# A bidirectional DeltaNet and S5 layer on one core: gate and branch tiles moved between the steps of the S5 blocks, and two branch stages made one

## The chip, the cores and the metric

One core of a Trainium2 chip runs the whole layer in one launch. The metric is the device time of the launch in microseconds. The engines are called PE (TensorE), DVE (VectorE), ACT (ScalarE), POOL (GpSimd) and SP (SyncE, which issues most transfers); a queue called ACTq or SPq in the profile is the instruction queue of that engine. All times below are in microseconds unless marked ns.

## What is computed

1280 tokens of 1024 channels (1024 of the sample, 256 of the prompt) go through one layer. Cut to what the change touches:

```
proj = h @ w_in                                  # qkv, z, b, a, u, gate_a, gate_b
o    = gated_delta(...)                          # 8 heads, two directions
y_a  = o @ w_br_a
y_s  = gelu(s5_fwd(u) + s5_bwd(u) + d * u)       # 64 groups of 16 channels, 64 complex states
y_s  = y_s * sigmoid(y_s @ w_glu + b_glu)
y_b  = y_s @ w_br_b
out  = (sigmoid(gate_a) * y_a + sigmoid(gate_b) * y_b) @ w_out
x    = x + gt1 * out                             # then the SwiGLU part and the last norm
mod  = silu(cond) @ w_ada + b_ada                # six shifts, scales and gates, two conditions
```

## The kernel before

Everything is kept with channels on the 128 partitions and the 1280 tokens along the free dimension. A weight product works on tiles: a tile is 1024 rows by 128 columns of a weight, loaded as f32 (`load_tile`, line 168), split into a bf16 high part by ACT (`split_high`, line 174) and a bf16 low part by POOL (`split_low`, line 179), and multiplied by PE in 72 instructions (`multiply_part`, line 190): 8 slices of 128 rows, three passes (high by high, high by low, low by high), and columns of 512, 512 and 256 tokens, 24 instructions for each of these three chunks of tokens. Two tiles, slot 0 and slot 1, form a pair. Loads, splits and products of a slot wait for one another by semaphores (`w_loaded`, `w_high`, `w_low`, `tile_done`, `tile_read`), so that the split of the next tile of a slot runs while PE multiplies the other slot. Each engine runs its instructions in the order in which they are written.

The phases follow one another: the input with its norm, the decays (`phase_decays`), the heads, S5, branch a, branch b, and the tail (output product, SwiGLU, last norm).

In `phase_decays` PE first multiplies the decay weights (line 656), then, between the steps of the decays, 16 products of adaLN rows (`ada_products`, line 279), whose 1 MB loads (line 271) share three slots; a slot is free when its product is done.

`phase_s5` has two parts. The first multiplies eight tiles of u, and beside them DVE works out the parameters: powers of the state's decay (`pa_re`, `pa_im`), the angle of a chunk of 8 tokens (`e1`), the factors of B and C. PE turns B and C between the first pair of u and the other three (lines 1517, 1527). The second part runs over 16 blocks of four groups. A sequence is cut into chunks of 8 tokens, 128 of the sample and 32 of the prompt. For each block:

- POOL makes tables of the cosine and sine of every chunk's angle by doubling, seven levels from 1 to 64 chunks (lines 1766 to 1781), for the next block; it starts when DVE has finished a block.
- DVE makes the input tables `wt` (lines 1878 to 1881) and the output tables `cc` and `cq` (1889 to 1895).
- PE turns `wt` (1794), ACT copies it into `w1` and `w2` (1850 to 1852), PE multiplies the chunks of u (1803), once for each direction, and makes kernel rows from `cc` (1813 to 1815); ACT copies these (1855), and SP spreads them into a Toeplitz block `m` by eight small transfers (1728).
- For each direction DVE rotates the products by the table (1904, 1905, 1910), runs eight scans (1919), and rotates back into `pq` (1925).
- PE forms the outputs from `m`, `cc` and `cq` (1821 to 1825), ACT copies them out of PSUM (1858), SP stores them.

After the last block SP loads one token of u for each direction (1752), from which the new states are worked out.

`phase_branch_a` multiplies, for each of 8 column tiles, the tile of gate_a and the tile of w_br_a, and beside them loads a slice of y and u, adds d * u, and forms the gelu. `phase_branch_b` multiplies 8 tiles of w_glu, and then, for each of 8 column tiles, the tile of gate_b and that of w_br_b; DVE and ACT form the merged rows. The tail loads x (2081) and begins with w_out.

Of the kernel before, what the change touches and what calls it, by code (L numbers as in the profile page):

```python
# [19 lines left out]
P = 128  # L20
# [30 lines left out]
NC5 = NC5_S + NC5_P  # L51
# [47 lines left out]
def setup(nc, ins, outs, consts, ctx):  # L99
# [49 lines left out]
    K.scratch_u = nc.dram_tensor("scratch_u", [KT, P, L5, NC5], F32, kind="Internal").ap()  # L149
    K.scratch_y = nc.dram_tensor("scratch_y", [KT, P, L5, NC5], F32, kind="Internal").ap()  # L150
# [59 lines left out]
def sources(K):  # L210
# [5 lines left out]
        "branch_a": (lambda j, slot: cols(w["w_br_a"], j, P, 0) if slot else cols(w["w_in"], j, P, GA0), KT),  # L216
        "glu": (lambda j, slot: cols(w["w_glu"], j, 2 * P, slot * P), KT),
        "branch_b": (lambda j, slot: cols(w["w_br_b"], j, P, 0) if slot else cols(w["w_in"], j, P, GB0), KT),
# [373 lines left out]
def phase_decays(K):  # L592
# [3 lines left out]
    with ExitStack() as st:  # L596
# [27 lines left out]
        with K.nc.Block() as block:  # L624
# [25 lines left out]
            def _(pe):  # L650
                pe.wait_ge(s_wl, 1)
                for j, out in ((0, pb), (1, pa)):
                    for k in range(KT):
                        for v, a in ((0, 0), (0, 1), (1, 0)):
                            for c0, cn in CHUNKS:
                                mm = pe.matmul(out[0:64, c0:c0 + cn], wp[:, j, v, k, :], K.hn[:, a, k, c0:c0 + cn],
                                               start=(k, v, a) == (0, 0, 0), stop=(k, v, a) == (KT - 1, 1, 0))
                    mm.then_inc(s_mm, 1)
                for n in range(KT, KT + 4):
                    ada_products(K, pe, n, acc)  # L660
# [4 lines left out]
                for n in range(KT + 4, 2 * KT):  # L665
# [4 lines left out]
                mm.then_inc(s_tr, 1)  # L670
                pe.wait_ge(s_dve, 8)
# [4 lines left out]
                ada_turn(K, pe, 1, trm)  # L676
                for n in range(2 * KT, 3 * KT):
# [36 lines left out]
            def _(dve):  # L714
                dve.wait_ge(s_par, 64)
                dve.wait_ge(s_mm, 2)
                dve.tensor_scalar(s_row[:, :], pa[0:64, 0:T], par[:, 0:1], None, ALU.add).then_inc(s_dve, 2)
                dve.wait_ge(s_act, 1)
# [20 lines left out]
                ada_rows(K, dve, 1, acc)  # L739
# [13 lines left out]
                ada_store(K, dve, 1, trm)  # L753
# [607 lines left out]
def phase_branch_a(K, mg, opairs, ys):  # L1361

    q0 = K.q
    K.q += KT
    with ExitStack() as st:
        sg = K.sb("a_sg", [P, T], stack=st)
        y = K.sb("glu_y", [P, L5, NC5], stack=st)
        u = K.sb("glu_u", [P, L5, NC5], stack=st)
        g = K.sb("glu_g", [P, T], stack=st)  # L1370
        out = [K.ps(f"a_out{s}", [P, 1536], st) for s in range(2)]
        s_o = [K.sem(f"a_o_in_{h}") for h in range(H)]
        s_sg, s_mg = K.sem("a_gate"), K.sem("a_mg")
        s_in, s_v, s_g, s_hi, s_lo = (K.sem("glu_" + n) for n in ("in", "sum", "gelu", "high", "low"))
        with K.nc.Block() as block:  # L1375
            @block.sync
            def _(sync):
                def load_y(j):
                    sync.wait_ge(s_g, j + 1)
                    sync.sem_inc(K.pulse, 1)  # L1380
                    for dst, src in ((y, K.scratch_y), (u, K.scratch_u)):
                        sync.dma_start(dst[:, :, :], src[bass.ds(j, 1)].rearrange("o p t c -> (o p) t c")).then_inc(s_in, 16)

                for h in range(H):
                    sync.dma_start(opairs[:, :, h, :], K.scratch_o[h]).then_inc(s_o[h], 16)
                load_y(0)
                with sync.Fori(1, KT) as j:
                    load_pair(K, sync, q0 + j, "branch_a", j)
                    load_y(j)
                load_pair(K, sync, q0 + KT, "glu", 0)  # L1390

            @block.gpsimd
            def _(pool):
                with pool.Fori(1, KT) as j:
                    low_pair(K, pool, q0 + j, "branch_a")
                low_pair(K, pool, q0 + KT, "glu")

            @block.tensor
            def _(pe):
                with pe.Fori(0, KT) as j:  # L1400
                    multiply_tile(K, pe, q0 + j, 0, out[0], K.hn)
                    for h in range(H):
                        pe.wait_ge(s_o[h], 16)
                    multiply_tile(K, pe, q0 + j, 1, out[1], opairs)

            @block.scalar
            def _(act):
                act.sem_inc(s_g, 1)
                with act.Fori(0, KT) as j:
                    act.wait_ge(s_mg, j + 1)  # L1410
                    wait_tile(K, act, q0 + j, 0)
                    act.activation(sg[:, :], out[0][:, 0:T], ACT.Sigmoid).then_inc(K.tile_read[0], 1)
                    split_high(K, act, q0 + j + 1, 0)
                    act.wait_ge(s_v, j + 1)
                    act.wait_ge(s_lo, j + 1)
                    act.activation(g[:, :].rearrange("p (c t) -> p t c", t=L5), y[:, :, :], ACT.Gelu_apprx_tanh).then_inc(s_g, 1)
                    act.wait_ge(s_g, j + 2)
                    act.activation(one(ys[:, 0, :, :], j), g[:, :], ACT.Copy).then_inc(s_hi, 1)
# [931 lines left out]
```

## Time and profile before

| | |
|---|---|
| median of 3 runs | 4470.55 (4466.76 to 4479.29) |
| profiled execution | 4473.08 |
| its span, first to last instruction | 4471.3 |
| PE busy in the span | 3638.4 (81%) |
| DVE busy | 2032.6 (45%) |
| ACT busy | 1086.6 (24%) |
| POOL busy | 944.5 (21%) |
| mean granted clock of TensorE | 0.897 |

An idle time is put down to the instruction that released the engine. By stage, the span is: input and decays to 186, heads to 2075, S5 parameters to 2243, S5 blocks to 2867, branches a and b to 3417, tail to 4471.

### The profile page before, as it was taken

The numbers are of one execution on the slowest core, as the hardware profiler recorded it, in microseconds if no ns is written. First come the engines' busy times: TensorE is split into PE (matmuls) and PEld (weight loads), VectorE is DVE, ScalarE is ACT, GpSimd is POOL, SyncE is SP. The second block draws the span as 40 slices with busy tenths as digits, with TensorE's granted clock in tenths as the row PEclk, the third lists the DMA queues.
The fourth block names the chain that finished last, engine by engine and source line by source line (L and its number), as shares of the span: only waits on it lengthen the run. The fifth ranks groups of instructions, "written<-read, shape, count | busy, mean of one in ns | idle before, by whom it ended". The sixth has DMA issues, their size and how long they took to land. (4 is left out here: it accounts for less than half of the span.)

```text
span 4471.3 us, 60897 instructions
## 1 busy us (share of the span) xinstructions
PE 3638.4 (81%) x22318; PEld 2423.4 (54%) x22318; DVE 2032.6 (45%) x3325; ACT 1086.6 (24%) x1719; POOL 944.5 (21%) x1059
## 2 busy tenths in 40 slices
PE   5789797979797979796844444699999899999997
PEld 2367574748484848484444444455454455555554
DVE  4366565656565656565279999312311211111112
ACT  3132323232323242322211111133211421111112
POOL 2100000000100001010187787011112311111112
PEclk8799898989898989898867767799999999999998
DMA  5400000000000000002111111321112111111111
GB/s 205 152 5 11 19 11 19 11 19 11 19 11 19 11 19 11 19 1 67 59 26 25 27 28 25 98 84 61 38 42 85 32 39 38 42 38 38 43 33 62
DMA packets 224361, 178.64 MB, mean 40 GB/s; under 512 B 23965, under 2 KB 211406, under 8 KB 220838
## 3 DMA queue, kind: packets, MB, share of 16 engines
q1 hardware_dynamic: 217974, 153.94, 11.7%
q10 hardware_dynamic: 4608, 11.54, 0.7%
q0 software_dynamic: 1584, 10.49, 0.6%
q8 instruction: 132, 2.16, 0.2%
q14 instruction: 63, 0.52, 0.0%
HBM read 144.39 MB, written 27.33 MB: 38 GB/s over the span
## 5 line engine op out<-in xcount | busy, mean ns | idle before, releaser
L179 POOL TENSOR_TENSOR w_pair<-w_raw,w_pair 128x1024 bf16<-128x1024 f32 (+1 forms) x156 | 345.7, 2218 | 2461.0 <-ACT w_pair L174 2461.0
L190 PE MATMUL t_out<-hn,w_pair 128*128 128x512 bf16 (+1 forms) x3168 | 575.8, 345 | 13.5 <-DVE hn L2247 10.6
L190 PE MATMUL bank<-hn,w_pair 128*128 128x512 bf16 (+1 forms) x2304 | 487.0, 360 | 86.0 <-ACTq L1219 71.1
L190 PEld LDWEIGHTS t_out<-hn,w_pair 128*128 128x128 bf16 x3168 | 310.9, 98 | 278.1 <-issue 18.4
L190 PE MATMUL t_out<-ys,w_pair 128*128 128x512 bf16 (+1 forms) x2160 | 401.2, 349 | 24.4 <-DVE ys L2268 14.8
L190 PEld LDWEIGHTS bank<-hn,w_pair 128*128 128x128 bf16 x2304 | 224.9, 102 | 294.6 <-issue 129.7
L190 PEld LDWEIGHTS t_out<-ys,w_pair 128*128 128x128 bf16 x2160 | 213.9, 99 | 210.0 <-issue 32.0
L174 ACT ACTIVATE w_pair<-w_raw 128x1024 bf16<-128x1024 f32 x156 | 162.9, 1050 | 419.0 <-PE t_out L190 321.4
L1821 PE MATMUL s_banks<-u_block,m_block 128*128 128x160 f32 x128 | 41.0, 414 | 250.0 <-DVEq L1927 250.0
L2264 DVE TENSOR_TENSOR t_sq<-t_out,t_sq 128x1280 f32<-128x1280 f32 x22 | 32.8, 1492 | 463.7 <-PE t_out L190 463.7
L190 PE MATMUL b_out<-ys,w_pair 128*128 128x512 bf16 (+1 forms) x1152 | 210.8, 345 | 4.0 <-PEq L1375 4.0
L1035 PE MATMUL bank<-xi,mt 128*128 128x128 f32 x1600 | 197.2, 281 | 20.3 <-DVE xi L1289 13.3
L1048 PE MATMUL bank<-xti,vi 128*128 128x128 f32 x1600 | 206.1, 275 | 0.0
L1035 PEld LDWEIGHTS bank<-xi,mt 128*128 128x128 f32 x1600 | 188.9, 196 | 25.9 <-DVE xi L1289 15.0
L1048 PEld LDWEIGHTS bank<-xti,vi 128*128 128x128 f32 x1600 | 192.1, 192 | 0.0
L1161 ACT ACTIVATE gk<-bank,head_scalars 128x128 f32<-128x128 f32 x160 | 45.6, 368 | 535.2 <-PE bank L1027 535.2
L1087 PE MATMUL bank<-u,kd 128*128 128x256 f32 x320 | 108.2, 421 | 79.4 <-DVE u L1319 79.4
L2036 DVE SCALAR_TENSOR_TENSOR merged<-t_out,mod,merged 128x1024 f32 (+1 forms) x48 | 40.2, 880 | 287.7 <-PE t_out L190 267.6
L1299 DVE TENSOR_TENSOR vi<-bank,level_t 128x512 f32<-128x512 f32 x200 | 138.2, 691 | 69.5 <-PE bank L1035 64.4
L1043 PE MATMUL bank<-vi,xti 128*128 128x128 f32 x1280 | 169.3, 275 | 0.0
L1323 DVE SCALAR_TENSOR_TENSOR state<-state,head_carry,bank 128x128 f32<-128x128 f32 x320 | 97.0, 345 | 158.2 <-PE bank L1087 158.2
L1821 PEld LDWEIGHTS s_banks<-u_block,m_block 128*128 128x128 f32 x128 | 30.0, 273 | 253.9 <-DVEq L1927 253.9
(366 smaller groups left out, 6305.8 us busy)
## 6 DMA issues: line engine op xcount, KB each, us to landing
w_raw<-in_w_in SPq DMA_DIRECT2D x56, 512.0 KB, 4.1
w_ada_rows<-in_w_ada SPq DMA_DIRECT2D x24, 1024.0 KB, 6.4
w_raw<-in_w_gu SPq DMA_DIRECT2D x44, 512.0 KB, 3.8
w_raw<-in_w_down SPq DMA_DIRECT2D x16, 512.0 KB, 4.0
scratch_x<-x_t POOLq DMA_DIRECT2D x1, 5120.0 KB, 18.0
scratch_o<-o_pair ACTq DMA_DIRECT2D x8, 640.0 KB, 3.7
scratch_u<-u_rows ACTq DMA_DIRECT2D x8, 640.0 KB, 2.9
u_block<-scratch_u SPq DMA_DIRECT2D x128, 40.0 KB, 1.8
```

The lines of the kernel that those rows point to most:

```text
L174: act.activation(K.w_pair[:, slot, 0, 0:kt, :], K.w_raw[:, slot, 0:kt, :], ACT.Copy).then_inc(K.w_high, 1)
L179: pool.tensor_tensor(K.w_pair[:, slot, 1, 0:kt, :], K.w_raw[:, slot, 0:kt, :], K.w_pair[:, slot, 0, 0:kt, :], ALU.subtract).then_inc(K.w_l ...
L190: mm = pe.matmul(out[:, c0:c0 + cn], K.w_pair[:, slot, w, k, :], x[:, a, k, c0:c0 + cn], start=i < 3, stop=i >= 9 * kt - 3)
L1035: mm = pe.matmul(b[:, t, :], mt[:, 4 * g + t, :], xi[:, 4 * g + t, :], start=True, stop=True)
L1043: mm = pe.matmul(b[:, t, :], xti[:, 4 * g + t, :], vi[:, 4 * g + t, :], start=True, stop=True)
L1048: mm = pe.matmul(b[:, t, :], vi[:, 4 * g + t, :], xti[:, 4 * g + t, :], start=True, stop=True)
L1087: pe.matmul(b[:, 0:2 * P], kd[:, t, :], u[:, i % 2, :, :].rearrange("p d c -> p (d c)"), start=True, stop=True).then_inc(rd.full, 1)
L1161: act.activation(gk[:, 4 * g + t, :], b[:, t, :], ACT.Copy, scale=hs[:, 3, 4 * g + t:4 * g + t + 1])
L1299: dve.tensor_tensor(vi[:, grp(g), :], b, level[:, l, :].unsqueeze(1).to_broadcast([P, 4, P]), ALU.mult).then_inc(rd.free, 1)
L1323: dve.scalar_tensor_tensor(out=state[:, q, d, :], in0=state[:, q, d, :], scalar=hc[:, d, t:t + 1], in1=b[:, d * P:(d + 1) * P], op0=ALU.mu ...
L1821: pe.matmul(o, m[:, g, :], u[:, slot, g, :], start=True, stop=False, skip_group_check=True)
L2036: i = dve.scalar_tensor_tensor(out=v, in0=out[:, a:a + n], scalar=K.mod[:, bass.ds(j + gate * KT, 1), c:c + 1].rearrange("p o c -> p (o c) ...
```

## The change

It touches four places.

1. `phase_decays`: the 16 products of adaLN rows are issued by PE between the decay weights' products (one after every second slice), and the rest between the later steps; the turned rows are stored earlier.
2. S5 parameters: the start state is turned back by the angle of 64 chunks, for which DVE squares `e1` six times; the copies `pb_re` and `pb_im` go. One column is put between sample and prompt (`PROMPT5`).
3. S5 blocks: the loops are written out. POOL makes tables of 64 chunks instead of 128 (six levels), one block ahead; ACT copies them into tables by position (`positions`: mirrored, with the angle counted from the middle) and makes a table of multipliers with zeros at sequence starts (`decays`), so that DVE runs one scan over all four groups and both sequences for each direction. `cq` is copied from `cc` by ACT. Input tables are made a block ahead. The S5 products use six banks; the other two take weight tiles: 16 tiles of gate_a and gate_b, then 8 of w_br_a, cut into 64 gaps of 48 units (a unit is one instruction of 256 columns), four gaps to a block. ACT puts each finished chunk through a sigmoid, or copies it, and stores it in `scratch_g`. Four gaps (40 to 43) stay empty while the heads' outputs are loaded into `hn`. The token loads at the end are issued in the last block.
4. `phase_branches` takes the place of `phase_branch_a` and `phase_branch_b`: it loads y and u slice by slice, forms the gelu, and multiplies the first two tiles of w_glu slice by slice as it comes; then the other six tiles of w_glu and the 8 of w_br_b. The gates and y_a are loaded from `scratch_g`; POOL multiplies gate_a by y_a. x is loaded here instead of in the tail.

The core of the diff:

```
 # phase_decays, PE
+                        if k % 2:
+                            ada_products(K, pe, KT + 4 * j + k // 2, acc)
-                for n in range(KT, KT + 4):
-                    ada_products(K, pe, n, acc)
 ...
 # S5 parameters, DVE
+                    for _ in range(6):
+                        tt(W(5), W(2), W(2), ALU.mult)
+                        tt(W(6), W(3), W(3), ALU.mult)
+                        tt(W(7), W(2), W(3), ALU.mult)
+                        dve.drain()
+                        tt(W(2), W(5), W(6), ALU.subtract)
+                        dve.tensor_scalar(W(3), W(7), 2.0, None, ALU.mult)
+                        dve.drain()
 ...
 # S5 blocks: where a tile's instructions stand, and the order on PE, ACT, DVE and POOL
+        def start_unit(t, c, i=0):
+            return 120 * t + 48 * c + (1 if c == 2 else 2) * i + (IDLE if t >= GATES else 0)
 ...
+                for b in range(NB):                       # PE
+                    chunk_inputs(b, 0)
+                    fill(4 * b + 1)
+                    if b < NB - 1:
+                        turn_weights(b + 1)
+                    chunk_inputs(b, 1)
+                    fill(4 * b + 2)
+                    fill(4 * b + 3)
 ...
+                    outputs(b)
+                    fill(4 * b + 4)
+                    if b < NB - 1:
+                        kernel_rows(b + 1)
 ...
+                for b in range(NB):                       # ACT
+                    store_chunks(4 * b + 1)
+                    if b < NB - 1:
+                        weights(b + 1)
+                    store_chunks(4 * b + 2)
+                    store_chunks(4 * b + 3)
+                    if b < NB - 1:
+                        positions(b + 1)
+                        decays(b + 1)
+                    read_y(b)
+                    store_chunks(4 * b + 4)
+                    if b < NB - 1:
+                        second_outputs(b + 1)
+                        rows(b + 1)
 ...
+                for b in range(NB):                       # DVE
+                    if b < NB - 1:
+                        input_tables(b + 1)
+                    scan(b, 0)
+                    scan(b, 1)
+                    if b < NB - 1:
+                        output_tables(b + 1)
 ...
+                def scan(b, d):
+                    dve.wait_ge(s.pos, b + 1)
+                    dve.wait_ge(s.x, 2 * b + d + 1)
+                    dve.tensor_tensor(into, xb[:, :, 0:NC5], tcs[:, d, :, 1 - d:1 - d + NC5], ALU.mult)
+                    dve.tensor_tensor(gt[:, :, :], x2b[:, :, 0:NC5], tss[:, d, :, 1 - d:1 - d + NC5], ALU.mult).then_inc(s.xread, 1)
+                    dve.tensor_tensor(into, into, gt[:, :, :], ALU.add)
 ...
+                    dve.tensor_tensor_scan(o, r, v, 0.0, ALU.mult, ALU.add)
 ...
+                for b in range(NB):                       # POOL
+                    more = b + 1 < NB
+                    if more:
+                        first_angles(b + 1)
+                        for n in (1, 2):
+                            double(n)
+                    low_parts(4 * b + 1)
+                    if more:
+                        for n in (4, 8):
+                            double(n)
+                    low_parts(4 * b + 2)
+                    if more:
+                        double(16)
+                    low_parts(4 * b + 3)
+                    if more:
+                        double(32)
+                        pool.drain().then_inc(s.tables, 1)
+                    low_parts(4 * b + 4)
 ...
+                def kernel_rows(b):                       # PE
+                    pe.wait_ge(s.cc, b + 1)
+                    if b:
+                        pe.wait_ge(s.yread, b)
 ...
+                def positions(b):                         # ACT
+                    act.wait_ge(s.tables, b + 1)
+                    if b:
+                        act.wait_ge(s.pq, b)
 ...
 # one stage of branches, PE
+                for k in range(KT):
+                    pe.wait_ge(s_slo, k + 1)
+                    for slot in range(2):
+                        multiply_part(K, pe, slot, out[slot], ys, 9 * k, 9)
+                for j in range(1, KT // 2):
+                    for slot in range(2):
+                        multiply_tile(K, pe, q0 + j, slot, out[slot], ys)
+                for j in range(KT):
+                    if j == 0:
+                        pe.wait_ge(s_lo, KT)
+                    multiply_tile(K, pe, q1 + j // 2, j % 2, out[j % 2], ys2)
 ...
+                def load_slice(k):                        # SP
+                    if k >= 2:
+                        sync.wait_ge(s_g, k - 1)
+                    for dst, src in ((y, K.scratch_y), (u, K.scratch_u)):
+                        sync.dma_start(dst[k % 2], src[k]).then_inc(s_in[k % 2], 16)
```

## Rows read from the trace of the kernel before

**Rows 1.** Busy time by stage: bounds, length, engines (instructions), clock, DMA share, GB/s.
```profile
2075.00:2243.00 168.00, 127.34 (x646) 68.90 (x645) 58.21 (x156) 37.96 (x77) 17.09 (x8) 0.84 0.29 87
2243.00:2867.00 624.00, 290.35 (x1674) 265.42 (x1675) 525.54 (x901) 61.84 (x129) 446.50 (x752) 0.69 0.11 24
2867.00:3417.00 550.00, 526.57 (x2881) 283.54 (x2882) 123.57 (x72) 144.54 (x116) 91.87 (x40) 0.98 0.22 67
```

**Rows 2.** Waits, 2260 to 2830: who waited for whom, total, times, longest.
```profile
PE s_banks L1821 <- DVEq L1927: 250.0, 16, 17.4
```

**Rows 3.** Timeline of POOL: start, length, engine, line, operation; a weight split, one block's tables.
```profile
2113.07 2.12 POOL L179 TENSOR_TENSOR w_pair<-w_raw,w_pair 128x1024 bf16<-128x1024 f32 x1 [109.58 <-ACT w_pair L174]
...
2510.64 0.11 POOL L1766 MEMSET rot_cos<- 128x8 f32 x1 [5.40 <-DVEq L1927]
...
2524.13 0.30 POOL L1775 TENSOR_TENSOR rot_tmp<-rot_cos 128x64 f32<-128x64 f32 x1
...
2533.73 1.04 POOL L1775 TENSOR_TENSOR rot_tmp<-rot_cos 128x512 f32<-128x512 f32 x1
...
2546.80 0.11 POOL L1766 MEMSET rot_cos<- 128x8 f32 x1 [5.40 <-DVEq L1927]
```

**Rows 4.** Timeline of PE: the first w_br_b pair's start and the tail's first tile.
```profile
3196.55 16.00 PE L190 MATMUL b_out<-hn,w_pair 128*128 128x512 bf16 x72 [8.05 <-DVE ys L2019]
...
3416.89 43.41 PE L190 MATMUL t_out<-ys,w_pair 128*128 128x512 bf16 x229 [9.64 <-PEq L160]
```

**Rows 5.** Timeline of PE: transposes of a block, outputs of the last block, its end.
```profile
2482.40 1.04 PE L1794 MATMUL s_banks<-ident,wt 128*128 128x128 f32 x8
...
2827.04 0.90 PE L1821 MATMUL s_banks<-u_block,m_block 128*128 128x160 f32 x2 [9.67 <-DVEq L1927]
...
2829.86 0.66 PE L1821 MATMUL s_banks<-u_block,m_block 128*128 128x160 f32 x2
...
2831.44 0.43 PE L1821 MATMUL s_banks<-u_block,m_block 128*128 128x160 f32 x2
...
2832.80 0.43 PE L1821 MATMUL s_banks<-u_block,m_block 128*128 128x160 f32 x2
...
2852.90 7.16 PE L1838 MATMUL s_banks<-rot_tmp,ones 1*128 1x512 f32 x8 [18.58 <-DMA rot_tmp<-scratch_u]
```

**Rows 6.** Timeline of DVE: a long scan of the decays, then one S5 block.
```profile
135.14 2.81 DVE L723 TENSOR_TENSOR_SCAN c_row<-restart_t,s_row 32x1280 f32<-32x1280 f32 x1
...
2516.47 0.76 DVE L1891 TENSOR_TENSOR cq<-c,pa_re 128x576 f32 x1
...
2526.02 0.69 DVE L1904 TENSOR_TENSOR g_tmp<-s_banks,rot_cos 128x512 f32<-128x512 f32 x1 [2.14 <-PE s_banks L1803]
...
2539.20 0.69 DVE L1904 TENSOR_TENSOR g_tmp<-s_banks,rot_cos 128x512 f32<-128x512 f32 x1
...
2546.29 0.28 DVE L1925 TENSOR_TENSOR pq<-g_scan_p,rot_sin 128x128 f32<-128x128 f32 x1
```

**Rows 7.** Groups of ACT in the S5 blocks: count, busy, mean ns, idle before.
```profile
L1850 ACT ACTIVATE w<-s_banks 128x512 f32<-128x512 f32 x32 | 19.4, 608 | 12.1 <-PE s_banks L1794 10.8
```

**Rows 8.** Timeline of branch a: gelu of a slice, loads of the next, DVE's sum.
```profile
2892.53 2.52 ACT L1416 ACTIVATE glu_g<-glu_y 128x1280 f32<-128x1280 f32 x1
...
2895.75 0.38 SPq L1382 DMA_DIRECT2D glu_u<-scratch_u  x1
...
2900.98 1.55 DVE L1427 SCALAR_TENSOR_TENSOR glu_y<-glu_u,vec,glu_y 128x1280 f32<-128x1280 f32 x1 [1.44 <-DMA glu_u<-scratch_u]
```

**Rows 9.** Timeline of the S5 parameters: one small DVE operation, PE's second transposes.
```profile
2104.45 0.29 DVE L1571 TENSOR_TENSOR e_cos<-s_w 128x128 f32<-128x128 f32 x1
...
2133.91 1.97 PE L1517 MATMUL s_bank<-ident,bn 128*128 128x128 f32 x8 [9.32 <-DVE s_b L1655]
```

**Rows 10.** Timeline of the decays: SP's adaLN loads, PE's last decay product.
```profile
125.10 41.97 SPq L271 DMA_DIRECT2D w_ada_rows<-in_w_ada  x13
...
149.78 4.63 PE L674 MATMUL pb<-end_diag,ones 64*128 64x512 f32 x6 [1.45 <-DVE cum L744]
```

More of the change, by code:

```diff
@@ L670, in _ @@
                 mm.then_inc(s_tr, 1)
+                for n in range(2 * KT + 3, 2 * KT + 6):
+                    ada_products(K, pe, n, acc)
                 pe.wait_ge(s_dve, 8)
@@ L675, in _ @@
                 mm.then_inc(s_tr, 1)
[L676 to L677 removed]
+                for n in range(2 * KT + 6, 3 * KT):
                     ada_products(K, pe, n, acc)
@@ L1356, in _ @@
                 head(H - 1, False)
[L1361 to L1418, printed above, removed]
-                    split_high(K, act, q0 + j + 1, 1)
-            @block.vector
-            def _(dve):
-                dve.sem_inc(s_mg, 1)
-                dve.sem_inc(s_lo, 1)
-                with dve.Fori(0, KT) as j:
-                    dve.wait_ge(s_in, 32 * j + 32)
-                    dve.scalar_tensor_tensor(out=y[:, :, :], in0=u[:, :, :], scalar=K.s5_d[:, bass.ds(j, 1)], in1=y[:, :, :],
-                                             op0=ALU.mult, op1=ALU.add).then_inc(s_v, 1)
-                    dve.wait_ge(s_hi, j + 1)
-                    dve.tensor_tensor(one(ys[:, 1, :, :], j), g[:, :], one(ys[:, 0, :, :], j), ALU.subtract).then_inc(s_lo, 1)
-                    wait_tile(K, dve, q0 + j, 1)
-                    dve.wait_ge(K.tile_read[0], q0 + j + 2)
-                    dve.tensor_tensor(one(mg, j), out[1][:, 0:T], sg[:, :], ALU.mult).then_inc(s_mg, 1)
-                    dve.wait_ge(s_mg, j + 2)
-                    dve.sem_inc(K.tile_read[1], 1)
@@ L1493, in phase_s5 @@
             with nc.Block() as block:
-                stream(K, block, [("u", KT // 2, q0)], "branch_a", before=parameters)
+                stream(K, block, [("u", KT // 2, q0)], "gates", before=parameters)
                 @block.tensor
@@ L1744, in _ @@
[L1744 to L1752 removed]
+                        sync.dma_start(sy[t][:, b * GB:(b + 1) * GB, :], y[t * P_S5:(t + 1) * P_S5, :, :]).then_inc(s.y_out, 16)
@@ new lines, in decays, with weights @@
+                def decays(b):
+                    if b:
+                        act.wait_ge(s.pq, b)
+                    for d in range(2):
+                        for g in range(GB):
+                            j = b * GB + g
+                            i = act.activation(decay[:, d, g, :], keep[:, d, :], ACT.Copy, scale=r8[:, d, j:j + 1])
+                    i.then_inc(s.decay, 1)
+                def weights(b):
+                    act.wait_ge(s.wtr, b + 1)
+                    if b >= 2:
+                        act.wait_ge(s.x, 2 * b - 2)
+                    for d in range(2):
+                        v = turned[:, d, :, :]
+                        act.activation(w1[:, b % 2, d, :, :], v, ACT.Copy)
+                        act.activation(w2[:, b % 2, d, :, 0:64], v[:, :, 64:P], ACT.Copy)
+                        c = act.activation(w2[:, b % 2, d, :, 64:P], v[:, :, 0:64], ACT.Copy, scale=-1.0)
+                    c.then_inc(s.w, 1)
@@ new lines, in _ @@
+                weights(0)
+                positions(0)
+                store_chunks(0)
+                second_outputs(0)
+                rows(0)
+                for b in range(NB):
[12 more added lines that the diff above has]
+                        rows(b + 1)
@@ new lines, in phase_branches @@
+        yy = [tmp[:, 2, :], tmp[:, 3, :]]
+        y = [yu[:, i, 0, :, :] for i in range(2)]
+        u = [yu[:, i, 1, :, :] for i in range(2)]
+        g = sg
+        parts = lambda j: tmp[:, 2:5, :] if j % 2 else tmp[:, 5:8, :]
+        s_in = [K.sem("glu_in_0"), K.sem("glu_in_1")]
+        s_v, s_g, s_shi, s_slo = (K.sem("glu_" + n) for n in ("sum", "gelu", "high", "low"))
+        s_y, s_hi, s_lo = (K.sem("b_" + n) for n in ("y", "high", "low"))
+        s_parts = [K.sem("b_parts_0"), K.sem("b_parts_1")]
@@ new lines, in _ @@
+                for k in range(KT):
+                    q, slot = q0 + k // 2, k % 2
+                    if k >= 2:
+                        act.wait_ge(s_y, k - 1)
+                    wait_tile(K, act, q, slot)
+                    act.activation(sg[slot], out[slot][:, 0:T], ACT.Sigmoid, bias=K.b_glu[:, k:k + 1]).then_inc(K.tile_read[slot], 1)
+                    split_high(K, act, q + 1, slot)
+                    act.wait_ge(s_y, k + 1)
+                    act.activation(ys2[:, 0, k, :], yy[slot], ACT.Copy).then_inc(s_hi, 1)
```

665 lines of the change are left out of this document (419 added, 246 removed).

## The prediction

> **What bounds the kernel now.** I read the busy times by stage first, then the waits and the order of instructions inside the two stages that the change rewrites. Times in us. In the S5 blocks (2243 to 2867, 624 us) TensorE (PE) is busy 290 and VectorE (DVE) 526 [rows 1]. PE's longest wait there is the output product, 250 us in 16 blocks for the end of DVE's scans, and POOL's tables start 36.2 apart, each time on DVE (2510.64, 2546.80) [rows 2, 3]: a block is DVE's chain, with POOL's tables of the next block beside it. Right behind lie 550 us (2867 to 3417) in which PE is busy 527 [rows 1]: 40 weight tiles of 1024 x 128, back to back, 527/40 = 13.2 each; their records end into each other a little, so I take 13.1. So one stage leaves PE free for over 300 us while DVE is full, and the next one uses nothing but PE. The change lays the second over the first; what it can win is read from how much of each is left over.
>
> **The S5 blocks.** *PE's work.* 24 of the 40 tiles move here: 24 x 13.1 = 314. A gap of 48 units is 48/120 of a tile, 5.25. In the last old block five output products of 160 columns take 1.36 at full clock (2831.44 to 2832.80) [rows 5], 0.27 each; a block has 16 input and 20 output products, 9.8. Eight transposes are 1.0 [rows 5]. The kernel rows, four groups of 256 columns, are by columns 4 x 0.43 = 1.7. Together 12.5, and with four gaps 33.5 a block. PE's floor for the stage is 314 + 16 x 12.5 = 514.
>
> *Does DVE fit under it?* Tables: 12 operations where 18 were (the third product pair is now a copy on ACT), 0.76 each [rows 6], 9.1. One direction took 7.4 with POOL idle (2539.20 to 2546.57) [rows 6]. Now it is three operations of 640 elements (0.8), one scan of 648 in place of eight, two products (0.8 each) and a copy. A scan over a full multiplier tensor ran 1280 elements in 2.81 [rows 6], so 1.4; with drains a direction is 5.9. Sum 9.1 + 11.8 = 21, against 33.5. In block time (0 = first input products): inputs 0 to 2.2, gap, transposes, second inputs 8.5 to 10.7, two gaps to 21, outputs to 26.4, gap to 31.7, kernel rows to 33.5. DVE scans from 2.2 and 10.7 and ends near 17; the outputs want it at 21. Four of slack.
>
> *POOL.* Beside DVE six of the seven table levels took 23.1 (2510.64 to 2533.73); the last three of them, mostly beside DVE's waits and PSUM reads, 9.6, and an operation of 64 elements 0.30 [rows 3]. Smaller ones need no more, so the six are at best some 16.6. The seventh level and the copy of B go. Added: 1.5 weight splits a block of 2.12 [rows 3], 3.2. So 20 to 26, under 33.5.
>
> *ACT, and what is queued behind its waits.* Copies of 512 elements take 0.61 [rows 7]. By elements the ten position copies are 3.1, decays 1.6, reading y 0.8, weights 2.4, the second outputs 2.6, rows 1.0, tile and a half 5: 16.5, under 33.5. But ACT's order makes a chain: the position copies wait for POOL's tables, and reading y, which kernel rows wait for, stands behind them. POOL's last level stands behind a split when a tile ends in a block's third gap. That happens in blocks 1, 4, 6, 9 and 12. From 21.0: chunk copy 0.6, high split 1.1 (1024 elements), low split 2.1, last level 4.5 (9.6 shared over three levels by their lengths), positions 3.1, decays 1.6, y 0.8: 34.8 against 31.7, with semaphores a stall of 4. Other blocks lose nothing to 1. I take 4 x 4 = 16 and 9 for the rest and for DVE beside a split.
>
> *The empty gaps.* Gaps 40 to 43 hold no products while the eight heads' outputs (5.2 MB) are loaded into hn. Block 9 still has its 36, block 10 then runs on its own chain: 2.2, 1.6, inputs 2.2, two directions, near 15, outputs, one gap, rows: 27. PE's work in both is 46, so 17 are lost. The Toeplitz copies of block 10 are queued on SP behind the heads' transfers; they have until 15.
>
> *Ends.* Before block 0 tables come first: 5 lost, and the first scan waits for POOL's whole table and ACT's copies, and with them the copy that PE's second transposes want: 6. At the end, PE waited 18.6 for two token loads after the last block [rows 5]; they are now issued early in block 15 behind that block's work. Left are four narrow products (3.7) and 9 for copying, storing y and the barrier.
>
> Sum: 514 + 16 + 9 + 17 + 11 + 4 + 9 = 580, against 624: **-44**.
>
> **One stage in place of two.** Of the 40 tiles 16 stay, 8 of w_glu and 8 of w_br_b. The first two of w_glu can't start before the gelu. They run slice by slice as y arrives. A slice is two loads of 0.64 MB; in the old loop DVE had both 5.2 after the second issue [rows 8] (2895.75 to 2900.98). Then 1.55 on DVE, gelu 2.5 [rows 8] (in two parts 2.7), a copy, a subtraction. Two buffers: a buffer's turn is 5.4 + 1.6 + 2.7 = 9.7, so 4.9 a slice, the bounds being ACT's gelu and copy, 3.9, and no overlap, 9.7. First slice gelu'd at 11, eighth at 45, its halves and products 7 more: pair done at 52 (bounds 45 to 86). Both its tiles end together, so nothing covers the next split: sigmoid 1.5 by elements, splits 1.1 and 2.1, with a table load about 6. Then 6 tiles 79, the old wait of 8 before w_br_b [rows 4] (its end is the same four operations), 8 tiles 105, 2 more for PE's lower clock at the start, and 9.6 to the next stage as before [rows 4]. 262 against 550: **-288**. The gate products on POOL, the loads of parts and of x lie under tiles of 13: the latest part load waits for a merge two tiles back. ACT no longer changes its table twice per tile; that lay beside PE and is worth nothing.
>
> **Before the blocks.** The turned start state adds to DVE's chain of parameters: six squarings of five operations on 128 elements, and some 14 more with a reciprocal; at 0.29 less overlap [rows 9], with drains 6 x 1.3 + 4 = 12, less four copies, 1.4. PE waits for that chain (9.3 on its second group of transposes) [rows 9] and has three tile pairs behind it, so nothing hides it: **+10** (8 to 13). The second copy of u per tile lies beside a tile.
>
> **The adaLN rows.** 13 loads of 1 MB start at 125.10, once PE frees their slots, and last 42 [rows 10]. With products between the decay products the slots come free 26 earlier. What is late next is the decay chain, moved back by 8 products of 1: its last product (149.78 + 4.63) [rows 10] ends at 163, 4 before the old last load is even issued, and that load's landing, 4 or more, drops out of the tail, while two row products move behind the chain: **-8** (0 to -15).
>
> **Sum.** -44 - 288 + 10 - 8 = -330. The profiled execution's span is 4471.3, its own time 4473.1 (1.8 around the span), 2.5 above the median of 4470.6. 4471.3 - 330 + 1.8 - 2.5 = 4140.6; I say **4140**.
>
> **Rivals.** *DVE and POOL take turns.* Where POOL ran its levels of 256 and 512 elements, one direction of DVE took 13.2 (2526.02 to 2539.20) instead of 7.4 [rows 6]. If every POOL operation excludes every DVE operation with both inputs in SBUF, a block needs 9.1 + 1.6 + 2.8 + 3.2 = 16.7 on DVE and 16.6 + 3.2 = 19.8 on POOL, 36.5 one after the other, and with chains around it about 38: the blocks are then 4.5 longer, 16 x 4.5 = 72, 4212. Against it: in the table stretch DVE kept 0.76 while POOL's small operations slipped between. The Trainium skill, SBUF - State Buffer, Who interferes with whom, has this as an exclusive lock that a two-SBUF-input DVE operation and a reading GpSimd operation hold for their whole length, the other one blocked; the trace agrees for the long levels, but not for the small ones, which cost DVE nothing; by the page for all of them the result is the 4212 of this rival.
> *The lower clock.* The granted clock is 0.69 in the old blocks [rows 1], and after 9.7 idle an output group took 2.82 (2827.04 to 2829.86), twice the 1.36 later [rows 5], so it ran at 1.2 GHz and then at 2.4. If the new stage also had 0.69, PE's 514 would be 514 x 0.98/0.69 = 730: 4356. Against it: idle is now 12% of the stage, not half, and stretches as dense as that show 0.98 [rows 1].
> *Loads of slices don't overlap:* pair done at 86 instead of 52, 4174.
> *The fills lengthen the chain instead of filling it.* PE works in order. If each gap stood on the way between a product and the scan that wants it, a block would be the old 36.2 plus four gaps, 57: 912 and 28 for the ends, 360 more than forecast, 4500, slower than before. It decides once DVE's end, now 4 ahead of the outputs, lies behind them by as much as the gaps are long in every block; the schedule above speaks against it.
> *It doesn't do what it says:* the stages overlap less, for instance because splits on POOL come late and PE waits for tiles; that gives between 4212 and 4356.
>
> **How the numbers follow.** Forecast with its own spread (4100 to 4180) 0.58; DVE and POOL in turn (4180 to 4240) 0.19; slices unlapped 0.06; clock or late splits 0.08; series 0.03; better than 4100 (stalls hidden, 25 to 45 of the 66 us that I put on top of PE's floor not there) 0.06. The range 4095 to 4215 leaves out less than 2 in 10. A difference of 0.3% (13 us) is about what a measurement of this kernel can tell from no change. Faster by more: 0.96; within: 0.01; slower by more: 0.03.
>
> **What will show it.** Right: in the S5 stage PE busy above 85%, granted clock above 0.9, blocks 33 to 36 apart except near 36 and 27 for the two around the empty gaps; output products hardly waiting for DVE; PE's kernel rows waiting for ACT in the five named blocks; a first pair of w_glu of about 50. Wrong: output products waiting on DVE in every block (lock), blocks above 38, a clock near 0.7, fills waiting for POOL's weight splits, a first pair of 80.

## The result and the profile after

| kernel | median, us | runs | ratio to before (95% interval) | profiled span |
|---|---|---|---|---|
| before | 4470.95 | 4 (4466.76 to 4479.29) | 1 | 4471.3 |
| changed | 4229.2 | 4 (4224.29 to 4229.91) | 0.9455 (0.9438 to 0.9471) | 4227.4 |

The change makes the kernel 242 us faster, where 330 had been forecast: 4229 against 4140, and 14 above the end of the range. To see where the 88 are, cut both traces at the same events: the first product of the heads, the last product of the heads, POOL's first table of the S5 blocks, ACT's first table load of the branches, and the first product of the tail ([rows 4] has that one for before). First the instruction timeline of the kernel before (start, duration, engine, line, operation; in brackets the idle time ahead of it and what ended it):

```profile
187.86 12.38 PE L190 MATMUL bank<-hn,w_pair 128*128 128x512 bf16 x57 [10.56 <-POOL w_pair L179]
2070.71 4.64 PE L1105 MATMUL bank<-kd,ones 128*128 128x512 f32 x6 [3.57 <-ACT kd L1205]
2243.04 0.11 POOL L1766 MEMSET rot_cos<- 128x8 f32 x1 [0.71 <-DVEq L1929]
2866.84 1.28 ACT L1412 ACT_TABLE_LOAD   x1 [31.70 <-DVEq L1423]
```

and that of the changed kernel:

```profile
182.59 15.60 PE L195 MATMUL bank<-hn,w_pair 128*128 128x512 bf16 x72 [10.68 <-POOL w_pair L184]
2066.53 4.63 PE L1114 MATMUL bank<-kd,ones 128*128 128x512 f32 x6 [3.57 <-ACT kd L1214]
2251.50 0.11 POOL L1789 MEMSET rot_cos<- 128x8 f32 x1 [0.46 <-POOLq L1426]
2918.21 1.28 ACT L2231 ACT_TABLE_LOAD   x1 [6.86 <-PEq L165]
3174.49 1.03 PE L195 MATMUL t_out<-ys,w_pair 128*128 128x512 bf16 x2 [8.41 <-PEq L2158]
```

| stretch | before | after | difference | forecast |
|---|---|---|---|---|
| up to the heads | 187.9 | 182.6 | -5.3 | -8 |
| heads | 1882.9 | 1883.9 | +1.1 | 0 |
| S5 parameters and u | 172.3 | 185.0 | +12.6 | +10 |
| S5 blocks | 623.8 | 666.7 | **+42.9** | **-44** |
| branches | 550.1 | 256.3 | -293.8 | -288 |
| tail | 1054.4 | 1052.9 | -1.5 | 0 |
| sum | 4471.3 | 4227.4 | -243.9 | -330 |

Five of the six come out within 6 us of the forecast, and their errors nearly cancel (-0.9 together). The S5 blocks miss by 87, which is the whole difference. Busy time by stage of the changed kernel, the answer to [rows 1] (stretch, length, then busy time and instructions of PE, PE's weight loads, DVE, ACT and POOL, the granted clock, DMA share and rate):

```profile
2067.00:2251.00 184.00, 132.40 (x652) 71.02 (x651) 67.49 (x194) 40.52 (x87) 17.11 (x8) 0.81 0.27 80
2251.00:2918.00 667.00, 562.09 (x3401) 395.50 (x3401) 379.75 (x442) 252.13 (x545) 350.76 (x665) 0.90 0.28 74
2918.00:3174.00 256.00, 218.35 (x1152) 114.71 (x1152) 116.54 (x64) 79.49 (x66) 67.32 (x24) 0.93 0.45 157
3174.00:4227.00 1053.00, 995.87 (x5460) 542.21 (x5460) 155.00 (x150) 206.58 (x189) 206.97 (x89) 0.97 0.14 41
```

In the blocks PE is now the busiest engine, DVE fell from 526 to 380, and the lower clock is gone (0.90, not 0.69). Still PE stands idle for 105 of 667. Who waits for whom in that stage (engine, what it writes, line, what it waited for; us in total, times, longest):

```profile
POOL w_pair L184 <- ACT w_pair L179: 237.3, 24, 16.9
DVE g_in L2081 <- PE s_banks L1873: 237.0, 29, 17.7
ACT pos_cos L1965 <- POOLq L1825: 128.1, 14, 11.0
PE s_banks L1887 <- ACT y_block L2012: 74.9, 14, 11.3
PE s_banks L1902 <- DVE pq L2099: 9.6, 1, 9.6
```

The output products' wait for DVE, 250 us in the kernel before [rows 2], is down to 9.6, once, in the block with the empty gaps. DVE has slack: 237 us of waiting for PE. In its place PE's kernel rows (L1887) wait for ACT's copy of y (L2012) 14 times, 75 us in all. ACT in turn waits 128 us for POOL's tables (L1965), and POOL 237 us for the high halves of weight tiles (L184), that is, for PE to end a tile. PE waits for ACT, ACT for POOL and POOL for PE: a ring. One turn of it, in block 2 (blocks are counted from 0 throughout):

```profile
2367.16 2.14 POOL L184 TENSOR_TENSOR w_pair<-w_raw,w_pair 128x1024 bf16<-128x1024 f32 x1 [14.09 <-ACT w_pair L179]
2371.28 1.56 POOL L1798 TENSOR_TENSOR rot_tmp<-rot_cos 128x64 f32<-128x64 f32 x1
2381.89 0.89 POOL L1798 TENSOR_TENSOR rot_tmp<-rot_cos 128x256 f32<-128x256 f32 x1
2386.70 0.73 POOL L1801 TENSOR_TENSOR rot_sin<-rot_tmp 128x256 f32<-128x256 f32 x1
2387.58 0.63 ACT L1965 ACTIVATE pos_cos<-rot_cos 128x512 f32<-128x512 f32 x1 [8.36 <-POOLq L1825]
2390.69 2.65 ACT L1982 ACTIVATE scan_decay<-scan_keep,r 128x162 f32<-128x162 f32 x8
2393.25 0.68 ACT L2012 ACTIVATE y_block<-s_banks 128x644 f32<-128x644 f32 x1
2394.08 0.59 PE L1887 MATMUL s_banks<-cc,bst 128*16 128x128 f32 x2 [4.82 <-ACT y_block L2012]
2397.58 3.35 PE L1873 MATMUL s_banks<-u_block,w 128*128 128x161 f32 x16
```

POOL stands 14 us idle with four table levels queued behind a split whose tile isn't done. The split runs, then the levels take 18 us (2369.3 to 2387.4); ACT copies positions and decays; only then comes y, and PE, which has waited 4.82. The wait costs twice. The granted clock in the gap ahead of the wait, in the kernel rows behind it, in the input products behind those, and in the gap's products that follow (same columns as above):

```profile
2384.00:2389.20 5.20, 5.20 (x37) 3.33 (x34) 1.31 (x2) 1.62 (x5) 3.29 (x4) 1.00 0.02 5
2394.10:2397.50 3.40, 3.40 (x24) 2.40 (x24) 0.00 (x0) 2.87 (x4) 1.67 (x1) 0.50 0.47 109
2397.60:2400.80 3.20, 3.20 (x18) 3.16 (x18) 0.00 (x0) 1.47 (x2) 2.63 (x16) 0.72 0.64 145
2401.00:2405.00 4.00, 4.00 (x20) 1.85 (x19) 3.73 (x5) 0.60 (x1) 3.58 (x10) 1.00 0.38 80
```

At 0.50, the lower of the two levels (1.2 GHz), the kernel rows take 3.50 (2394.08 to 2397.58). In block 0, without a wait, they took 1.95 (2265.97 to 2267.92).

### The profile page after: what moved, and what is told of

The parts are those of the page before. It is cut to its first block and busy times, and to the rows that moved or that the text cites. A ratio compares the mean times of both kernels' runs of the same rounds, so it can differ in the third digit from the quotient of the medians.

```text
span 4227.4 us, 59349 instructions
## 1 busy us (share of the span) xinstructions
PE 3593.6 (85%) x22319; PEld 2380.5 (56%) x22319; DVE 1889.9 (45%) x2896; ACT 1212.5 (29%) x2094; POOL 824.3 (19%) x955
## 5 line engine op out<-in xcount | busy, mean ns | idle before, releaser
L184 POOL TENSOR_TENSOR w_pair<-w_raw,w_pair 128x1024 bf16<-128x1024 f32 (+1 forms) x156 | 351.1, 2253 | 2331.7 <-ACT w_pair L179 2331.7
L1853 PE MATMUL s_banks<-hn,w_pair 128*128 128x512 bf16 (+1 forms) x1728 | 321.0, 345 | 0.0
L1853 PEld LDWEIGHTS s_banks<-hn,w_pair 128*128 128x128 bf16 x1728 | 169.7, 98 | 137.0 <-issue 2.7
L1044 PEld LDWEIGHTS bank<-xi,mt 128*128 128x128 f32 x1600 | 194.0, 201 | 29.4 <-DVE xi L1298 19.2
L195 PEld LDWEIGHTS b_out<-ys,w_pair 128*128 128x128 bf16 x1152 | 114.7, 100 | 140.5 <-issue 30.3
```

What stands on the lines that cost most here:

```text
L184: pool.tensor_tensor(K.w_pair[:, slot, 1, 0:kt, :], K.w_raw[:, slot, 0:kt, :], K.w_pair[:, slot, 0, 0:kt, :], ALU.subtract).then_inc(K.w_l ...
L195: mm = pe.matmul(out[:, c0:c0 + cn], K.w_pair[:, slot, w, k, :], x[:, a, k, c0:c0 + cn], start=i < 3, stop=i >= 9 * kt - 3)
L1044: mm = pe.matmul(b[:, t, :], mt[:, 4 * g + t, :], xi[:, 4 * g + t, :], start=True, stop=True)
L1853: mm = pe.matmul(out, K.w_pair[:, slot, wv, k, :], K.hn[:, a, k, c0:c0 + cn], start=i == 0, stop=i == 3 * KT - 1)
```

## Experiments

Three theories. **Queue**: the ring above is the whole shortfall; it is made by what stands ahead of what in POOL's and ACT's in-order queues, and opening it at any one place returns it. **Take turns** (the rival of the prediction): the table levels and DVE's products exclude each other, and the block's period is what the two need. **Clock**: PE is granted less in this stage whatever the waits.

| run | edit to the changed kernel | median, us | ratio to before (95%) |
|---|---|---|---|
| e1 | ACT reads y before positions and decays | 4152.9 | 0.9284 (0.9267 to 0.9300) |
| e2 | ACT reads y between positions and decays | 4195.0 | 0.9375 (0.9358 to 0.9391) |
| e3 | POOL makes all table levels, then splits | 4125.5 | 0.9228 (0.9211 to 0.9244) |
| e4 | DVE's tables left out after the first blocks | 4146.6 | 0.9274 (0.9257 to 0.9290) |
| e5 | e1 and e3 | 4127.7 | 0.9229 (0.9215 to 0.9243) |
| e6 | e3, and the start state turned last | 4113.0 | 0.9199 (0.9187 to 0.9212) |
| e7 | decay phase of the kernel before | 4244.6 | 0.9492 (0.9478 to 0.9507) |
| e8 | e3 and e4 | 4121.3 | 0.9212 (0.9197 to 0.9228) |

**e1: ACT's order.**

```diff
+                    read_y(b)
                     if b < NB - 1:
                         positions(b + 1)
                         decays(b + 1)
-                    read_y(b)
```

> The changed kernel with one exchange in ACT's order: reading y comes before the position copies and the decays of the next block instead of behind them. In the changed kernel PE's kernel rows wait 74.9 us in 14 times for the reading of y, and after such a wait the kernel rows take 3.5 where they took 1.95 in block 0. Theory 'queue' (that wait, predicted in five blocks, is in every block, because y's reading stands on ACT behind copies that wait for POOL's last table level, and it is the whole shortfall): the wait falls from 75 to under 10, kernel rows come back to about 1.95 (14 x 1.55 = 22 us) and the input products behind them by 0.7 each (10 us); ACT's copy of the kernel rows now comes later, so the transposes of the next block may wait some 1 us each. Total 4229 - 65 - 22 - 10 + 15 = about 4147 (4120 to 4170). Theory 'take turns' (DVE and POOL exclude each other and the block's period is what these two need, 38 or more): the wait moves to the position copies and the scans, the period stays near 40 and the time within 15 us of 4229. Theory 'clock' (PE is granted less in this stage whatever the waits): the wait goes but kernel rows stay at 3.5: about 4165 to 4180.

4152.9, 76 less. PE's waits in the blocks:

```profile
PE s_banks L1863 <- ACT k_rows L2006: 23.9, 14, 9.2
PE s_banks L1887 <- ACT y_block L2012: 0.9, 1, 0.9
```

The wait for y is gone. A smaller one took its place: ACT copies the kernel rows later now, and the next block's transposes (L1863), which use the same banks, wait for that (in the changed kernel once, for 6.4). *Take turns* (within 15 of 4229) and *clock* (4165 to 4180) both expected more time than this.

**e2: a smaller dose at the same place.**

```diff
                         positions(b + 1)
-                        decays(b + 1)
                     read_y(b)
+                    if b < NB - 1:
+                        decays(b + 1)
```

> The same place at a smaller dose: reading y is put between the position copies and the decays, so only the eight decays (2.65 us) no longer stand before it. 'Queue': the kernel rows' wait shortens by 2.65 in 14 blocks, 75 to about 38; kernel rows after a shorter wait still begin at the lower clock, so 0 to 12 more: 4229 - 37 = 4192 (4178 to 4196). 'Take turns': within 10 us of 4229, since POOL's tables end no earlier.

4195.0, 34 less for 2.65 us taken out ahead of y. The wait:

```profile
PE s_banks L1887 <- ACT y_block L2012: 44.7, 14, 8.7
```

So time follows what stands ahead of y on ACT nearly one to one: 30 of the wait and 34 of the total.

**e3: POOL's order.**

```diff
                         first_angles(b + 1)
-                        for n in (1, 2):
+                        for n in (1, 2, 4, 8, 16, 32):
                             double(n)
-                    low_parts(4 * b + 1)
...
-                    low_parts(4 * b + 4)
+                    for g in range(4 * b + 1, 4 * b + 5):
+                        low_parts(g)
```

> The changed kernel with POOL's order changed, ACT's as it was: POOL makes all six table levels of the next block first and splits the block's weight tiles behind them; in the changed kernel it stands 237 us in 24 waits for ACT's high halves, that is for PE to end a tile, with two or three table levels queued behind each. 'Queue': tables end some 8 us before reading y is wanted, the kernel rows' wait falls from 75 to under 10, with the clock 4229 - 70 - 30 = about 4130 (4105 to 4160); a split comes up to 15 later, but its tile is wanted only two and a half gaps after its buffer came free, so tiles don't wait. 'Take turns': the levels are as long (22 us or more in all) and now meet the scans and output tables of DVE, which then hold the output products: 4200 or above, with waits of the outputs for DVE's products. If the late splits are what matters, fills wait for POOL: 4230 or slower.

4125.5, 104 less. The busy times of 2300 to 2600 (columns as above), first of this kernel:

```profile
2300.00:2600.00 300.00, 300.00 (x1962) 210.82 (x1961) 205.87 (x245) 138.96 (x293) 186.73 (x374) 1.00 0.33 85
```

and of the changed kernel:

```profile
2300.00:2600.00 300.00, 260.60 (x1603) 182.46 (x1602) 172.14 (x197) 118.59 (x262) 160.66 (x298) 0.92 0.26 67
```

The input products and the kernel rows of the stage, grouped by line (busy time, mean ns of one, idle time ahead), in e3, where their lines are 1863 and 1877:

```profile
L1863 PE MATMUL s_banks<-u_block,w 128*128 128x161 f32 x512 | 79.0, 307 | 0.9 <-DVE c_tmp L2072 0.9
L1877 PE MATMUL s_banks<-cc,bst 128*16 128x128 f32 x128 | 24.5, 273 | 2.9 <-ACT y_block L2002 2.9
```

and in the changed kernel:

```profile
L1873 PE MATMUL s_banks<-u_block,w 128*128 128x161 f32 x512 | 85.9, 324 | 0.9 <-DVE c_tmp L2082 0.9
L1887 PE MATMUL s_banks<-cc,bst 128*16 128x128 f32 x128 | 37.6, 394 | 74.9 <-ACT y_block L2012 74.9
```

The first position copy of a block in the timeline of e3:

```profile
2397.68 0.64 ACT L1955 ACTIVATE pos_cos<-rot_cos 128x512 f32<-128x512 f32 x1 [0.46 <-ACT gate_ring L1938]
```

PE is busy for all 300 us at the full clock. ACT's copy follows its own last copy at once and no longer waits for POOL (8.36 in the turn above); kernel rows wait once, for 2.9, in the last block ahead of the empty gaps; with the wait the slow products went (37.6 to 24.5, 85.9 to 79.0): the clock was a result of the waits, so theory *clock* falls. Blocks stand 33.65 apart (2375.48 and 2409.11 are the starts of two). The stage, from POOL's first table at 2249.04 to ACT's table load at 2811.65, takes 562.6 instead of 666.7.

**e4: the share of contention.** `input_tables(b)` returns after its waits from block 1 on, `output_tables(b)` from block 2 on; that work is left out.

> The changed kernel with part of the work left out: DVE makes its input table for block 0 and its output tables for blocks 0 and 1 only, later blocks use these again; scans and all orders stay. In the changed kernel the last three table levels on POOL take 16 to 17 us a block, most of them beside these DVE operations; where DVE stood idle (block 10 and the first tables) the same three took 8.5 to 9.5. 'Queue' with contention as one of its links: the last level is 2.6 shorter where it alone stands behind a split, two or three levels are 4 to 7 shorter elsewhere, so the kernel rows' wait falls from 75 to some 10 to 25 and the total to 4229 - 57 - 20 = about 4152 (4130 to 4180). If contention is no link of it (the levels are long for another reason), levels stay at 16 and the time within 10 us of 4229.

4146.6, 83 less; the kernel rows' wait is 24.9 in 9 blocks:

```profile
PE s_banks L1887 <- ACT y_block L2012: 24.9, 9, 9.2
```

One operation of POOL's last level, grouped by line and form, 2300 to 2600 (busy time, mean ns), in the changed kernel:

```profile
L1798 POOL TENSOR_TENSOR rot_tmp<-rot_cos,rot_sin 128x256 f32<-128x256 f32 x8 | 8.6, 1074 | 0.0
```

in e4:

```profile
L1798 POOL TENSOR_TENSOR rot_tmp<-rot_cos,rot_sin 128x256 f32<-128x256 f32 x8 | 5.0, 631 | 0.0
```

and in e3:

```profile
L1798 POOL TENSOR_TENSOR rot_tmp<-rot_cos,rot_sin 128x256 f32<-128x256 f32 x9 | 13.2, 1469 | 0.0
```

With DVE's tables out of the way the operation takes 0.63 instead of 1.07. So contention of the two engines is a strong link of the ring: in POOL's old order most of the shortfall needs it. In e3 the same operation is longer still (1.47), and the mean one of that level takes 1.11 (1.00 in the changed kernel, 0.66 in e4), yet e3 is the faster kernel. That contention counts only while the tables are late is what e8 tests. How e4's block 2 runs, with a tile that ends in the same gap as in the turn above (the first and the last operation of POOL's last three levels, then the kernel rows):

```profile
2356.05 1.56 POOL L1798 TENSOR_TENSOR rot_tmp<-rot_cos 128x64 f32<-128x64 f32 x1
2366.33 0.73 POOL L1801 TENSOR_TENSOR rot_sin<-rot_tmp 128x256 f32<-128x256 f32 x1
2373.96 0.39 PE L1887 MATMUL s_banks<-cc,bst 128*16 128x128 f32 x2
```

Three levels take 11.0 there (2356.05 to 2367.06) where they took 16.2 in the turn above (2371.28 to 2387.43), and the kernel rows don't wait at all. (The expectation gives 8.5 to 9.5 for the three levels of the changed kernel where DVE stood idle. By the trace it is 11.2 for the first tables, 2261.58 to 2272.81, and 11.0 for those made around the start of block 10, 2684.55 to 2695.52.)

**e8: the same omission where the ring is open.**

> POOL's tables first, and with the same work left out as in the run without tables: DVE makes its input table for block 0 and its output tables for blocks 0 and 1 only. In POOL's old order this took 83 us. 'Queue' (DVE and POOL lengthening each other matters only through the kernel rows' wait): that wait is already gone, PE is busy all the time in blocks 1 to 8, so leaving the tables out is worth nothing more than the first block's ends, 4125.5 less 0 to 6: 4120 to 4127. 'Take turns' as a cost of its own: some tens of us less, under 4105.

4121.3: the omission that was worth 83 in POOL's old order is worth 4 in the new one, where the intervals of e3's and e8's ratios overlap. As a cost of its own, *take turns* falls.

**e5: both orders.**

> Both remedies at once: POOL makes all table levels before it splits weights, and ACT reads y before the position copies. 'Queue': each alone took the same wait away (75 us of the kernel rows' wait for reading y, to 2.9 and 0.9), so they don't add up: the time is that of POOL's order alone, 4125.5, within 6 us (if ACT's later copy of the kernel rows holds the transposes as it did with ACT's order alone, up to 8 above). If they were two separate causes, about 4050 (4125.5 less 76).

4127.7. Worth 76 and 104 alone, the two together are worth 102: two cuts through one ring.

**e6: the start state.** On top of e3, the lines from `dve.tensor_copy(W(2), e1[0][:, :, :])` to the two writes of `h0` move behind the last subtraction into `b2st`.

> POOL's order as in the run where POOL makes tables first, and one more edit: the turning of the start state (six squarings and what follows, 13.5 us on DVE from 2102.65 to 2116.1 in the changed kernel) moves from the middle of DVE's chain of parameters to its end, behind the last product of B, where DVE then has 88 us without work. Theory of the prediction (PE's second group of B transposes waits for that chain, 20.4 us instead of 9.3, and nothing behind it hides that): 11 to 13 us less than 4125.5, about 4113 (4108 to 4118), and that wait falls to about 7 to 9. Rival (the params term comes from ACT's or SP's new work, the second copy of u and the two more state loads): within 4 us of 4125.5.

4113.0, 12.5 less than e3. The second group of B's transposes in the changed kernel, with the first and last operation of the start state on DVE ahead of it:

```profile
2102.65 0.23 DVE L1546 COPY s_w<-e_cos 128x128 f32<-128x128 f32 x1
2115.48 0.59 DVE L1506 TENSOR_TENSOR h<-s_w 64x128 f32<-64x128 f32 x2
2141.40 1.97 PE L1450 MATMUL s_bank<-ident,bn 128*128 128x128 f32 x8 [20.42 <-DVE s_b L1614]
```

and in e6:

```profile
2125.91 1.98 PE L1450 MATMUL s_bank<-ident,bn 128*128 128x128 f32 x8 [8.77 <-DVE s_b L1589]
```

20.4 of waiting became 8.8, and the stretch from the last product of the heads (2062.71) to POOL's first table (2234.82) takes 172.1, as in the kernel before (172.3). So the params term was this chain. This version is the fastest of all: 8.0% below the kernel before, 2.7% below the changed one by the medians.

**e7: the decay phase undone.**

> The changed kernel with the decay phase of the kernel before put back: the products of the adaLN rows stand behind the decay products again. The prediction had -8 for this part (0 to -15); by the two traces the first product of the heads comes 5.3 us earlier. If that difference is this part's, the time is 4233 to 4235 and the first product of the heads is back at about 187.9; by the prediction's own number 4237.

```profile
187.91 12.29 PE L195 MATMUL bank<-hn,w_pair 128*128 128x512 bf16 x55 [10.69 <-POOL w_pair L184]
```

The first product of the heads is back at 187.91, as expected, so the gain ahead of the heads is this part's. Its size isn't as sharp as 5.3: in the traces of the other runs, all with the new phase, that product starts between 179.2 (e2) and 182.9 (e6), 5 to 9 earlier. The profiled span is 4235.0, 7.6 above the changed kernel's, the median 15 above; the runs themselves lie between 4236.8 and 4245.7. What the part is worth beyond that isn't settled by this.

## Why the prediction missed by 88 us

**The step that failed** is in the paragraph on ACT's queue: "POOL's last level stands behind a split when a tile ends in a block's third gap. That happens in blocks 1, 4, 6, 9 and 12 ... Other blocks lose nothing to 1." The mechanism and the order of its links were seen: tables, positions, decays, y, kernel rows. Where a tile ends in the third gap alone (blocks 1, 6 and 12) the size came out too: 4.1 of waiting each, 4 forecast. Wrong is that other blocks lose nothing to 1. A tile lasts two and a half gaps, so every block up to 14 but the one with the empty gaps has a tile that ends in its first three gaps, and POOL stands at each of them. After a tile ended in gap 1, four levels are still to come; after gap 2, two; after gap 3, one. The forecast took for granted that with an earlier tile end all is done in time. It isn't: after the split in block 2's gap 1 the levels need 18.1, and they end 30.9 after the block's start (2356.56 to 2387.4); in block 1 the split came 20.8 after the start, the single level ended 29.4 after it. From block 1 on every case ends at 29 to 32, and 6.4 of ACT's work follows (2387.58 to 2393.93; 5.5 in the forecast, which had 1.6 for the decays and not 2.65), so every one of these blocks loses: nine beside the five that were named, 45 of the 75. Of the five only four were priced; block 9, whose fourth gap is empty, waited longest, 11.3.

**The length that was mis-sized**, and the reason for the wrong count, is that of the last three levels. I took 9.6 for them, from a stretch of the kernel before in which DVE mostly waited or read PSUM [rows 3]. In the turn shown they take 16.2. Between 2300 and 2600 the changed kernel's mean operation of 64, 128 and 256 elements is 0.597, 0.776 and 0.996; with six operations each, 14.2 without the idle time between them. In e4 they are 0.475, 0.561 and 0.660, 10.2. And with the levels near the forecast's length, e4's wait falls back mostly on the forecast's list: 17.6 of it in the five named blocks, 7.4 in four others, none in the rest. That 16 had been forecast for the five is chance, since block 9 alone has 9.2. Levels that wait for PE's tile end fall into the time in which DVE ends its scans and makes its tables, and these tables are the part of the block that the 9.6 did not contain. The Trainium skill (SBUF - State Buffer, Who interferes with whom) says that "only the shared port pair causes contention, and it's an exclusive lock". The L1798 rows of the changed kernel and e4 (1.07 and 0.63) agree that the neighbour's work stretches the operation; that it is a lock they don't show. So what the *take turns* rival is built on was at work, but as a link of the ring. What the rival made of it, a period of 38 set by the two engines' sum, is not what happened: POOL's total (about 22 a block, forecast 20 to 26) and DVE's fit under PE, as e3 and e8 show.

**A term that was missing** is PE's clock behind such a wait. I had set aside the lower clock for the stage as a whole, and rightly (0.90), but gave nothing for the stretch behind a stall of 4 to 5 us, although [rows 5] show just that: an output group at half speed after 9.7 of idle. Here it was some 1.55 for the kernel rows in most of 14 blocks, about 21, and 85.9 - 79.0 = 7 for the input products.

Together: 75 of waiting where 16 were forecast, +59, and 28 for the clock: 87, the size of the miss. The 28 counts two groups only; by PE's busy time of the stage, 562.1 here and 528.5 in e3, it would be 34, so the sum is good to some 6 us. For the rest of the forecast stands e3: its stage takes 562.6, and the forecast without the 16 of stalls was 580 - 16 = 564.

**Right:** block period (33.65 in e3 against 33.5), PE's floor, DVE's slack, the two ends and the empty gaps (block 9 and 10 of e3 take 62.5 together, from 2577.37 to 2639.92, 63 forecast; one by one they are 31.4 and 31.2, not 36 and 27). The branches: pair, split and tiles in the changed kernel,

```profile
2930.79 9.18 PE L195 MATMUL b_out<-ys,w_pair 128*128 128x512 bf16 x36 [20.07 <-DVE ys L2253]
2966.73 3.42 PE L195 MATMUL b_out<-ys,w_pair 128*128 128x512 bf16 x18 [0.57 <-DVE ys L2253]
2973.46 6.84 PE L195 MATMUL b_out<-ys,w_pair 128*128 128x512 bf16 x29 [3.31 <-POOL w_pair L184]
```

has its first pair done 52 after the stage's start (2918.2 to 2970.2), as forecast; loads of slices do overlap, and a bound of 86 wasn't needed. The split behind the pair cost 3.3, not 6. The start state is +12.6 for +10, with 13.4 of DVE time (2102.65 to 2116.07) where 12 were forecast. The decay part is -5.3 for -8 (5 to 9 by all the traces); its last row product still waits for a load, 2.66 at 167.99 in the changed kernel.

**Of the rivals** none came true, though the time lies 17 above that of *take turns* and inside the span given for *it doesn't do what it says*. A time near a rival's is no evidence for it: no fill waited for a weight split, outputs waited for DVE once, and the wait that did appear stands in the prediction's own list, with five blocks where there are fourteen.

## What to carry to other kernels

When two kinds of work share an in-order queue, one with a due date far off (a weight split wanted two and a half gaps later) and one on the ring that sets the period (the next block's tables), put the second first: moving a few lines on POOL was worth 104 us. Check such a ring in every phase that two unequal periods can have against each other, not only in the phase that looks worst, and take the length of each link from a stretch in which the same neighbours run. A wait in the middle of dense matmuls costs more than its own length: here about 28 us for 75.

## Hardware, beyond what was expected

In the turn shown, PE ran at 1.00 ahead of a wait of 4.82, came back at 0.50 for the kernel rows (3.4 us), showed 0.72 over the next 3.2 and 1.00 behind that. The stage's mean of 0.90 looks harmless, and yet 28 us of the 667 are this.
